# Expert loop: the fourth gathered block's transposes stand between the two halves of the pair's scatter

## The reference

```
hg = jnp.einsum('td,edf->tef', x_b, w_gate)
hu = jnp.einsum('td,edf->tef', x_b, w_up)
return jnp.einsum('tef,efd->td', jax.nn.silu(hg) * hu * g_b[..., None], w_down)
```

## Time and profile before

| | us |
|---|---|
| median of 3 runs | 1851.6 |
| lowest and highest run | 1846.26 and 1856.39 |
| the profiled execution, its own time | 1852.87 |
| its span, first to last instruction | 1851.2 |

### The profile page before, as it was taken

The page is one execution under the profiler, slowest core; times in us unless marked ns, Lnnn a source line. Parts: engine busy times, 40 slices in busy tenths (PEclk is TensorE's granted clock), DMA queues, the critical chain, the costliest instruction groups (busy, mean ns, idle before and its releaser), DMA issues. The chain is left out here.

```text
span 1851.2 us, 28485 instructions
## 1 busy us (share of the span) xinstructions
PE 1582.0 (85%) x11520; PEld 1315.4 (71%) x11520; DVE 1008.6 (54%) x1482; ACT 678.8 (37%) x911; POOL 133.2 (7%) x238
## 2 busy tenths in 40 slices
PE   2898588779799993998647678999999999999996
PEld 1896276679799993895636567777777777777774
DVE  2444744156566535675438455565565666665653
ACT  1433321144454324361132333443444444444441
POOL 5000000000100000000003001001000000010000
PEclk9897578589899997997977779999999999999998
DMA  5340500024555470565005038888889888989880
GB/s 177 137 162 1 169 15 2 1 90 147 174 176 189 170 166 6 137 183 182 1 0 183 0 112 289 301 334 321 327 324 342 340 338 334 345 333 338 331 329 39
DMA packets 113218, 349.22 MB, mean 189 GB/s; under 512 B 9633, under 2 KB 33392, under 8 KB 96448
## 3 DMA queue, kind: packets, MB, share of 16 engines
q1 hardware_dynamic: 104224, 317.85, 47.8%
q0 software_dynamic: 8240, 27.40, 4.8%
q10 hardware_dynamic: 624, 2.16, 0.3%
HBM read 345.15 MB, written 2.23 MB: 188 GB/s over the span
## 5 line engine op out<-in xcount | busy, mean ns | idle before, releaser
L2706 DVE TENSOR_TENSOR weights_lo<-raw_weights,weights_hi 128x2048 fp32r<-128x2048 f32 x99 | 223.8, 2288 | 81.5 <-ACT weights_hi L2610 81.5
L2610 ACT ACTIVATE weights_hi<-raw_weights 128x2048 fp32r<-128x2048 f32 x99 | 185.5, 1912 | 22.2 <-DMA raw_weights<-in_w_gate 18.8
L517 PE MATMUL bank<-in_x_hi,in_w_hi 128*128 128x256 f32 (+2 forms) x472 | 139.0, 295 | 26.1 <-DVE in_w_lo L487 26.1
L2412 PE MATMUL bank<-x_hi,weights_hi 128*128 128x256 f32 x544 | 154.8, 285 | 0.0
L2413 PE MATMUL bank<-x_lo,weights_hi 128*128 128x256 f32 x544 | 154.6, 284 | 0.0
L2414 PE MATMUL bank<-x_hi,weights_lo 128*128 128x256 f32 x544 | 154.6, 284 | 0.0
L517 PE MATMUL bank<-in_x_hi,in_w_lo 128*128 128x256 f32 (+2 forms) x472 | 137.3, 291 | 0.0
L517 PE MATMUL bank<-in_x_lo,in_w_hi 128*128 128x256 f32 (+2 forms) x472 | 137.2, 291 | 0.0
L2492 PE MATMUL bank<-raw_weights,gathered_pair 128*64 128x512 f32 x512 | 113.4, 595 | 0.0
L517 PEld LDWEIGHTS bank<-in_x_hi,in_w_hi 128*128 128x128 f32 (+1 forms) x472 | 91.5, 194 | 28.2 <-DVE in_w_lo L487 26.9
L1475 PE MATMUL bank<-merge_x_hi,ffn_weights_hi 128*128 128x256 f32 x352 | 100.3, 285 | 11.1 <-PEq L457 11.1
(11 more groups left out here) (571 smaller groups left out, 3836.1 us busy)
## 6 DMA issues: line engine op xcount, KB each, us to landing
raw_weights<-in_w_gate SPq DMA_DIRECT2D x64, 1024.0 KB, 8.9
raw_weights<-in_w_up SPq DMA_DIRECT2D x64, 1024.0 KB, 9.3
raw_weights<-in_w_down SPq DMA_DIRECT2D x64, 1024.0 KB, 8.5
weight_ring<-in_w_in SPq DMA_DIRECT2D x18, 2048.0 KB, 9.7
mixer_memory<-in_w_ada SPq DMA_DIRECT2D x96, 256.0 KB, 3.8
weight_ring<-in_w_ffn_in SPq DMA_DIRECT2D x22, 1024.0 KB, 6.8
weight_ring<-in_w_ffn_out SPq DMA_DIRECT2D x5, 2048.0 KB, 8.2
weight_ring<-in_w_out SPq DMA_DIRECT2D x4, 2048.0 KB, 7.5
```

What stands on the lines that cost most here:

```text
L517: mm = T.matmul(bank[m % banks][0:w, 0:n], weights[:, k, :], x[:, r0 + k, :], start=(k == 0 and weights is hi and x is x_hi), stop=(k == r ...
L2412: T.matmul(out_, hi[:, d, cut], x_hi[:, d, :], start=(d == 0), stop=False)
L2610: S.activation(w_hi[:, n % 4, :], raw_w[:, k % RAW, :], ACT.Copy).then_inc(s_hi.sem, 1)
L2706: V.tensor_tensor(w_lo[:, n % 4, :], raw_w[:, k % RAW, :], w_hi[:, n % 4, :].bitcast(F32), ALU.subtract).then_inc(s_lo.sem, 1)
```

## The change

The pair's scatter is cut into its two halves. In PE's queue the four transposes of block 3 move from ahead of the scatter to between the halves. No instruction is added or taken away; the queues of the other engines are not touched. In the last step (`i` = 15) there is no block to gather and nothing changes.

```diff
+                def scatter_half(i, put, ready, half):
+                    pe.wait_ge(s_put.sem, 8 * i + 2)
+                    pe.wait_ge(s_ylo.sem, ready + half)
+                    for c in range(2):
+                        for y in (y_hi, y_lo):
+                            mm = T.matmul(bank[2 * c + half][:, :], put[:, i % 2, c * P:c * P + P], y[:, half * 512:half * 512 + 512],
+                                          start=False, stop=False, skip_group_check=True)
+                    return mm
+
                 def scatter(i, put, ready, done):
-                    pe.wait_ge(s_put.sem, 8 * i + 2)
-                    for half in range(2):
-                        pe.wait_ge(s_ylo.sem, ready + half)
-                        for c in range(2):
-                            for y in (y_hi, y_lo):
-                                mm = T.matmul(bank[2 * c + half][:, :], put[:, i % 2, c * P:c * P + P], y[:, half * 512:half * 512 + 512],
-                                              start=False, stop=False, skip_group_check=True)
-                    mm.then_inc(done.sem, 1)
+                    scatter_half(i, put, ready, 0)
+                    scatter_half(i, put, ready, 1).then_inc(done.sem, 1)
...
                     pair_down(i)
                     if i + 1 < STEPS:
                         gather(i + 1, 2)
+                    scatter_half(i, put_p, 4 * i + 3, 0)
+                    if i + 1 < STEPS:
                         gather(i + 1, 3)
-                    scatter(i, put_p, 4 * i + 3, s_pair_put)
+                    scatter_half(i, put_p, 4 * i + 3, 1).then_inc(s_pair_put.sem, 1)
```

## The result

The changed kernel takes 1866.74 us in the median of 8 runs (1858.5 to 1877.22), the kernel before 1851.53 us beside it (8 runs, 1840.9 to 1856.39). The ratio is 1.0085, with a 95% interval of 1.0053 to 1.0117: 15 us slower, where 6 were forecast. A second job gave 1.009 (1.0066 to 1.0114). The profiled execution, at 1858.5 us the fastest of its eight, shows less of the loss than a usual one does.

What follows compares the result with a forecast made beforehand. PE's queue was taken to bound the loop at 42.92 us a step; 0.47 cost less 0.07 gain gave 0.40 us in 15 steps, 6.0 us in all. Forecast median 1857.6 us, 0.32% slower, range 1850.5 to 1864.

Steps and rivals of the forecast that it cites:

- The stall that block 3 filled: PE between block 2's end and DVE's low part of the first output half; block 3's transposes nearly free there.
- PE's new idle time: PE idle before the pair's first scatter matmul, about 0.7 us in each of 15 steps.
- The insertion: Four transposes between the scatter's fourth and fifth matmuls: 0.92 us in place of 0.45, costing 0.47 us a step.
- The lateness of ACT against PE: ACT's copy of block 3 and the weight splits queued behind it, 1.12 us late relative to PE.
- The gain of 0.07 a step: Pair's first scatter half starts 0.09 us earlier, leaving 0.07 after its second matmul; bounds nothing to 0.15.
- the 0.06: Delay in us from DVE's end to PE's matmul at the single's second half, applied to the pair's first half.
- What is late next: Section following block 3's late copy to its waiters on all queues; found all covered, adding nothing to the sum.
- rival (d): Clock falls to 1.2 GHz behind PE's new idle time in each step: 35 us, 1892 us; chance 0.01.
- (b): Late indirect DMA becomes PE's bound at block 0: 7.5 us more, 1865 us; chance 0.07.
- (c): Each transpose between the halves pays its whole 0.274 us: 15.9 us in all, 1867.5 us; chance 0.02.
- (a): Nothing is lost: a stall elsewhere absorbs 0.40 us a step, or the first half starts sooner; 1851.6 us; chance 0.07.
- (e): Faster: first half starts at block 2's end as DVE's low part comes sooner; 3.8 us gained, 1847.8 us; chance 0.02.

Runs made afterwards that it cites:

- splits first: Changed kernel, with ACT's split and DVE's low part of piece n+7 made before block 3's copy and low part: 1856.65 us, ratio 1.0036.
- without the gathers: Changed kernel without the indirect DMAs of steps 1 to 15, step 0's rows used in all steps: 1854.31 us, ratio 1.0026.
- early row DMAs: Changed kernel, with POOL's three row DMAs issued ahead of its wait for silu: 1853.49 us, ratio 1.0014.
- before_late_rows: Kernel before, with POOL's row DMAs issued later, after the next low part of weights on DVE: 1888.64 us, ratio 1.0198.
- held splits: Kernel before, with ACT waiting for the end of the pair's scatter before the split of piece n+7: 1862.82 us, ratio 1.0089.
- block 3 last: Changed kernel, with block 3's transposes moved behind both halves of the pair's scatter: 1884.44 us, ratio 1.0154.

## Why the prediction was wrong

**What was right.** The stall that block 3 filled and its price outside the stall were as described; PE's new idle time is 0.50 us in the view, where about 0.7 was put. The insertion was put at 0.47 us, and 0.92 - 0.45 = 0.47 was measured. The lateness of ACT against PE was put at 1.12, and 1.11 was measured. With the collision held back in three ways the change costs 6.9 us (splits first), 6.7 (without the gathers) and 0.4 (early row DMAs, interval up to 6), against the 6.0 forecast. An undisturbed step went from the scatter's start to the next product in 2.38 us, forecast 2.4.

**The term that was mis-sized.** The gain of 0.07 a step from an earlier start of the scatter isn't there: it starts 0.15 us after DVE's end in both kernels. The lower end of my bounds for it, nothing, was the true value. It makes 1 us in all. I took the 0.06 from the single's second half, and the code says what sets that place apart: it had one wait, for `s_ylo`, while a first half waits for `s_put` and `s_ylo`. In five steps read in each kernel, a start 0.15 after DVE's end has a wait record of 0.051 us (`EVENT_SEMAPHORE`, at the line of the `s_ylo` wait) ahead of its weight load, and a start 0.06 after it has none. The changed kernel has the second wait in the single's second half too, and there 0.06 became 0.15. Block 3 has two waits as well, with the one for DVE written first, and starts 0.06 after DVE's end; no such record stands in the us before it in step 8. No run takes the wait away alone, so the cause is read from the traces and not shown by experiment.

**The step that failed** is the list of who waits, under "What is late next". For the late row DMAs and the gather I looked for one waiter, PE at block 0, and found it covered; that cover did hold (before_late_rows, with twice the lateness, has 2.3 us of it, in three steps). For the gate piece I looked at when SP may issue it, and rightly found this unchanged. What I didn't ask is what else is on the DMA engines while it flies. Its flight is the first link of the chain that ends in the scatter, and next to nothing covers it: in step 9 of the changed kernel the piece is 1.99 us late and PE waits 2.00 longer, and in step 10 of the kernel before 1.3 and 1.2. That step was in the trace that I read: the stall of 1.2 us of the earlier trace rows was a late gate piece, and I never asked what had made it.

```profile
1605.19 1.91 ACT L2610 ACTIVATE weights_hi<-raw_weights 128x2048 fp32r<-128x2048 f32 x1 [2.42 <-DMA raw_weights<-in_w_gate]
...
1609.82 0.71 PE L2446 MATMUL bank<-kept,gathered_rows 128*128 128x128 f32 x4 [1.23 <-DVE gathered_lo L2731]
```

Five steps of two kernels show the link. "Overlap" is the gather's last landing less the gate piece's issue, both worked out from the issues and the times to landing:

| kernel, step | second indirect DMA, issue + time to landing | gate piece's issue | overlap | gate piece's time to landing |
|---|---|---|---|---|
| changed, 3 | 1292.96 + 5.6 | 1297.86 | 0.7 | 4.7 |
| held splits, 2 | 1245.82 + 5.1 | 1250.20 | 0.7 | 4.7 |
| changed, 9 | 1554.75 + 5.5 | 1558.58 | 1.7 | 6.7 |
| held splits, 4 | 1333.14 + 5.4 | 1336.60 | 1.9 | 7.2 |
| held splits, 12 | 1685.63 + 6.0 | 1689.12 | 2.5 | 8.2 |

All 42 steps of three profiles (kernel before, changed kernel, held splits; steps 1 to 14) give the shape. In the 25 with an overlap of up to 1.1 us the piece lands in 4.7 to 4.9 us, with one 5.1, where there was no overlap. In the 13 from 1.26 to 1.54 it takes 4.8 to 6.3. In the 4 above 1.6 it takes 6.7 to 8.2. So the loss starts beyond about 1.1 us of overlap and then grows faster than the overlap. Overlap alone doesn't set it: two of the steps with 1.35 and 1.54 lost nothing (4.9 and 4.8), and there the gather itself took longest, 6.5 and 6.2 us. The kernel before stood close to this edge, with 0.7 to 1.1 us of overlap in five of its steps and more in three. That is why the small delay cost so much and why it falls on single steps. The Trainium skill has the rule that I should have weighed (DMA: Bandwidth & Descriptors, Issuing engines are not separate DMA queues): transfers issued by different engines run on the same 16 DMA engines and interleave. The traces agree: each of the landings above 5.1 us stands beside a gather.

**A second amplifier, which I had as rival (d) with a chance of 0.01.** In the held splits' step 4 the late piece leaves PE idle for 2.29 us, and the matmuls behind it start 0.43 apart in place of 0.23:

```profile
1348.41 1.01 PE L2446 MATMUL bank<-kept,gathered_rows 128*128 128x128 f32 x4 [2.29 <-DVE gathered_lo L2732]
1349.10 0.77 PE L2521 MATMUL bank<-expert_out_hi,put_pair 128*128 128x512 f32 x1
1349.67 0.63 PE L2521 MATMUL bank<-expert_out_lo,put_pair 128*128 128x512 f32 x1
1350.10 0.63 PE L2521 MATMUL bank<-expert_out_hi,put_pair 128*128 128x512 f32 x1
```

```profile
1346.90:1350.40 3.50, 1.99 (x7) 1.75 (x8) 3.16 (x6) 1.53 (x5) 0.00 (x0) 0.75 0.99 404
```

The granted clock over this stretch is 0.75: it was 1.00 up to the end of the idle time, and 0.54 from 1348.40 to 1351.80, so it fell from 2.4 to 1.2 GHz behind the stall. From the scatter's start to the next product it then takes 3.30 us in place of 1.90. The Trainium skill's warning that TensorE's clock falls when it idles (TensorE: Matmul & The Clock Gate, HAM oscillation) agrees with it. The price that I gave, a fall in every step after 0.7 us, was wrong: both profiled executions of the changed kernel have 1.00 over the whole loop, stalls of 2.50 and 3.22 us included. So the length of the stall alone doesn't decide it. The held splits have three falls in 14 steps, behind stalls of 2.00 to 3.15 us, at 1.4 to 1.5 us each; the splits-first kernel, with PE's queue as in the changed one, has one fall behind 1.87 us, at 1.6; block 3 last has five, at 1.4 to 2.7. Whether slower executions of the changed kernel lose time in this way too is not known, for no profile shows one.

**The rivals.** (b), the late gather, had the right culprit and the wrong victim, and a chance of 0.07. (c) is out: the four transposes between the halves take 0.61 us. (a) is out, for the change is slower with an interval clear of 1. (e) is out, for the first half starts 0.15 after DVE's end as before and DVE's operation still takes 0.68.

**The sum.** 15 us are some 7 for block 3's place in PE's queue (two runs, 6.9 and 6.7) and some 8 to 9 for late gate pieces (1865.61 - 1856.65 = 9.0). How much of the 8 to 9 are falls of the clock is open: the two profiles of the changed kernel have none.

## What to carry to other kernels

When a step is moved, follow its lateness through every queue down to the DMAs it ends up delaying, and then ask two things of each: who waits for it, and whose transfer is in flight at its new time. A transfer that heads the critical chain has no cover of its own, so what drifts into its flight beyond some 1 us was paid here in full, and in single steps, which a reading of one typical step doesn't show. Read the untypical steps of the kernel before as well: they show what is close to an edge. If a chain sets the end, shorten it rather than reorder around it: cutting one DVE operation in two, with the second half behind what PE waits for, gained more than moving the transposes could.

## What was not expected of the hardware

- A 1 MB load took 4.7 us from issue to landing beside the last 0.7 us of a gather of rows, at most 4.9 beside its last 1.1, and 6.7 to 8.2 us beside its last 1.7 to 2.5 us.
- A TensorE stall of 2.29 us (held splits) and one of 1.87 (splits first) were followed by a granted clock of 1.2 GHz; stalls of 2.50 and 3.22 us in the changed kernel's two profiles were not. Behind the fall the same matmuls started 0.43 us apart, not 0.23.
- A matmul that waited for the same DVE operation started 0.06 us after its end at one place (the single's second half) and 0.15 at another (the pair's first half). The first place went to 0.15 too in the changed kernel, which adds a second wait there.
